# Three attentions run one step deeper, with divisions ahead of side work and output products inside the last step

## What is computed

```python
def first_block(...):                       # attention over 512 keys, spatial gating, 16 experts
    k_all = concat([kl, kc]); v_all = concat([vl, vc])
    mix_l = concat([gqa_attend(ql, k_all, v_all), spatial_gating(hl, ...)])
    xl_new = xl + gt1 * (mix_l @ w_out)
    xl_new = xl_new + gt2 * expert_choice_ffn(modulate(xl_new, g_ffn, sh2, sc2), w_router, w1, w3, w2)
    return rmsnorm(xl_new, g_final)

def mla_swa_layer(x, ...):                  # "even"
    o_mla = causal_block_attention(qm, km, v_m)
    o_swa = sliding_window_sink_attention(q_s, k_s, v_s, sinks, alibi_slopes(SWA_HEADS))
    return x + (concat([o_mla, o_swa]) * silu(gate)) @ w_out

def fox_layer(x, ...):                      # "odd"
    o = causal_block_attention(q, k, v, log_cum=log_cum)
    return x + (o * silu(gate)) @ w_out

def reference(...):
    x = first_block(...)
    x = mla_swa_layer(x, ...); x = fox_layer(x, ...)
    return rms_norm(x, g_final)
```

## Time and profile before

| | us |
|---|---|
| median of three runs | 1386.92 |
| the runs | 1386.84, 1386.92, 1388.49 |
| the profiled execution | 1388.61 |
| its span in the trace | 1386.8 |

### The profile page before, as it was taken

The page is one execution under the profiler, slowest core; times in us unless marked ns, Lnnn a source line. Parts: engine busy times, 40 slices in busy tenths (PEclk is TensorE's granted clock), DMA queues, the critical chain, the costliest instruction groups (busy, mean ns, idle before and its releaser), DMA issues.

```text
span 1386.8 us, 15261 instructions
## 1 busy us (share of the span) xinstructions
PE 992.9 (72%) x6623; PEld 510.2 (37%) x6623; DVE 396.3 (29%) x954; ACT 239.4 (17%) x483; POOL 89.6 (6%) x129
## 2 busy tenths in 40 slices
PE   4998987666666665566566565666656798899987
PEld 3765842212121111111111111111111487899875
DVE  4756421011111100101011010101101455775584
ACT  3534210000000000000000000000000355643452
POOL 1300000000020000000000000000000044300030
PEclk9999989878887887977888877788877798999998
DMA  9996789999999999999999999999999552144411
GB/s 398 375 378 237 317 362 428 428 429 426 429 427 427 430 427 427 429 427 428 429 428 427 428 428 426 430 428 427 428 427 428 216 184 98 62 182 146 159 62 46
DMA packets 34771, 482.47 MB, mean 348 GB/s; under 512 B 3854, under 2 KB 3856, under 8 KB 5520
## 3 DMA queue, kind: packets, MB, share of 16 engines
q1 hardware_dynamic: 34240, 479.92, 82.7%
q10 hardware_dynamic: 288, 1.05, 0.2%
q0 software_dynamic: 176, 0.53, 0.1%
HBM read 480.43 MB, written 1.05 MB: 347 GB/s over the span
## 4 chain that ended last, share of the span: by engine, by line
DMA 55%; PE 33%; DVE 6%; ACT 3%; issue 1%; POOL 1%; SPq 0%; POOLq 0%; DVEq 0%; ACTq 0%
DMA ring<-in_t_w 52%; PE PS L508 8%; PE PS L1009 6%; PE PS L496 6%; PE PS L1055 3%; DMA ring<-in_t_e_a 2%; DMA ring<-in_t_mod 2%; ACT S L624 1%; PE PS L690 1%; PE PS L485 1%; PE PS L997 1%; PE PS L786 1%; POOL RR L466 1%; PE PS L1022 1%; PE PS L808 1%
## 5 line engine op out<-in xcount | busy, mean ns | idle before, releaser
L1009 PE MATMUL PS<-ring,S 128*32 128x512 f32 x2016 | 320.7, 770 | 213.4 <-DMA ring<-in_t_w 210.9
L1055 PE MATMUL PS<-ring,S 128*32 128x512 f32 x1008 | 168.7, 803 | 103.7 <-DMA ring<-in_t_w 94.8
L1009 PEld LDWEIGHTS PS<-ring,S 128*32 128x32 f32 x2016 | 63.0, 126 | 447.7 <-DMA ring<-in_t_w 329.4
L514 DVE COPY S<-PS 128x512 f32<-128x512 f32 (+2 forms) x47 | 32.1, 682 | 307.9 <-PE PS L1055 287.7
L508 PE MATMUL PS<-SR,RR 128*128 128x256 f32 x736 | 117.5, 285 | 1.2 <-DVE ab L1441 0.9
L1055 PEld LDWEIGHTS PS<-ring,S 128*32 128x32 f32 x1008 | 33.3, 130 | 223.0 <-DMA ring<-in_t_w 147.6
L508 PEld LDWEIGHTS PS<-SR,RR 128*128 128x128 f32 x736 | 103.8, 189 | 2.6 <-DVE ab L1441 1.2
L454 ACT ACTIVATE RR<-ring 128x1024 fp32r<-128x1024 f32 (+3 forms) x95 | 89.5, 1005 | 37.8 <-DMA ring<-in_t_e_a 18.1
L1557 DVE TENSOR_SCALAR S<-PS,KC 128x256 f32<-128x256 f32 x16 | 7.7, 483 | 287.0 <-PE PS L1039 287.0
L516 ACT ACTIVATE S<-PS 128x512 f32<-128x512 f32 (+2 forms) x50 | 27.9, 568 | 340.8 <-PE PS L485 335.9
L466 DVE TENSOR_TENSOR RR<-ring,RR 128x1024 fp32r<-128x1024 f32 (+2 forms) x76 | 84.1, 1154 | 8.5 <-ACT RR L454 8.5
(11 more groups left out here) (309 smaller groups left out, 986.5 us busy)
## 6 DMA issues: line engine op xcount, KB each, us to landing
ring<-in_t_w SPq DMA_DIRECT2D x189, 2048.0 KB, 31.3
ring<-in_t_mod SPq DMA_DIRECT2D x12, 2048.0 KB, 12.7
ring<-in_t_out SPq DMA_DIRECT2D x6, 2048.0 KB, 7.8
S<-in_t_w SPq DMA_DIRECT2D x3, 2048.0 KB, 12.2
ring<-in_t_e_g SPq DMA_DIRECT2D x2, 2048.0 KB, 7.8
ring<-in_t_o_q SPq DMA_DIRECT2D x2, 2048.0 KB, 7.8
ring<-in_t_o_k SPq DMA_DIRECT2D x2, 2048.0 KB, 8.8
ring<-in_t_o_v SPq DMA_DIRECT2D x2, 2048.0 KB, 8.2
```

Source lines behind the costliest of these rows:

```text
L514: lane.e.tensor_copy(dst, src).then_inc(*lane.mark(out_of(key), *names))
L1009: m = pe.e.matmul(PS[32 * j:32 * j + 32, b, :], expert_rows(2 * k + kk, e_, e_ + 1), place[name, e_, k][:, kk, 512 * j:512 * j + 512], sta ...
L1055: m = pe.e.matmul(PS[q:q + 32, b, :], HT[e_ % 2][:, 128 * s + 32 * j:128 * s + 32 * j + 32], place["w2", e_, j][:, s, 512 * dh:512 * dh + ...
```

## The change

Four things are changed, none of them what is computed:

1. In all three attentions the scores, maxima and exponents of step 0 stand ahead of the loop (in the last two ahead of the gates' first pieces, together with the first division), and in round n those of step n+1 stand behind the transposes, copies and division of step n-1 and n. In the even attention the first step's patterns get two buffers of their own (`even_p`).
2. On VectorE the division stands ahead of the side work, and `gate_finish` stands behind it instead of at the head of the round.
3. In the last round of the even attention one block of the second output product stands between transposes and outputs (`out2_part`); in the odd attention half a block of the third (`out3_part`).
4. The blocks of the second and third output product come in another order (OUT2, OUT3), and VectorE's additions follow it.

```diff
-    A2_PB = [reg(o, 512) for o in (2048, 2560, 3072, 9216)]
+    A2_PB = [reg(o, 512) for o in (6144, 6656, 3072, 9216, 2048, 2560)]
+    def even_p(n, r):
+        return A2_PB[2 + (2 * n - 2 + r) % 4 if n else r]
+    OUT2 = ((1, 0), (1, 1), (0, 0), (0, 1), (1, 2), (0, 2), (1, 3), (0, 3))
+    OUT3 = ((1, 0), (0, 0), (1, 1), (0, 1))
...
         side = beside()
+        scores(0)
         for n in range(9):
-            if n < 8:
...
-            turn(side)
             if n:
                 for g in range(2):
                     pe.wait_ge((1, "p", n - 1, g))
                     transposes(pe, (1, "t", n - 1, g), ALL6,
                                [PB[(2 * (n - 1) + g) % 4][:, 128 * s:128 * s + 128] for s in range(4)])
+            if n + 1 < 8:
+                scores(n + 1)
             turn(side)
+            if n == 0:
+                turn(side)
             if n and n % 2 == 0:
...
+            if n:
+                turn(side)
         rest(side)
...
+        def out2_part(half, n2):
+            pe.wait_ge(*[("e", "done", m_) for m_ in ((0, 1) if half else (2, 3))])
+            straight(pe, ("out2", n2, half), ("out2", n2 // 2), OT, n2 % 2, final=half == 0 and n2 % 2 == 1,
+                     ks=range(4 * half, 4 * half + 4))
+
+        scores_even(0)
         side = gate_matmuls(pe, "e", (1, 0), HE)
...
+            scores_even(n + 1)
             turn(side)
+            if n == len(A2):
+                out2_part(*OUT2[0])
             if n:
...
+            turn(side)
         rest(side)
-        for half in (1, 0):
...
+        for half, n2 in OUT2[1:]:
+            out2_part(half, n2)
...
+        def out3_part(i, h, ks):
+            key, ukey = ("out3", h, i), ("out3", h)
...
+            for k in ks:
+                pe.wait_ge(("split", ukey, k), ("o", "done", (1 if i else 0) if k < 4 else (2 if i else 3)))
...
+            scores_odd(n + 1)
             turn(side)
+            if n == len(A3):
+                out3_part(*OUT3[0], range(4))
...
+            turn(side)
         rest(side)
+        out3_part(*OUT3[0], range(4, 8))
+        for i, h in OUT3[1:]:
+            out3_part(i, h, range(8))
...
+        maxima(0)
         for n in range(9):
+            if n:
+                probabilities_out(dve, n - 1, 1)
+            if n + 1 < 8:
+                maxima(n + 1)
             if n < 8:
...
+            turn(side)
             turn(side)
...
+        dve.wait_ge("bias")
+        largest_even(0)
+        divide_even(0)
         late = []
         side = gate_dve(dve, "e", (1, 0), late)
...
         for n in range(len(A2) + 1):
+            if n:
+                turned_out(dve, "e", n - 1, 1, A2_PT, 2)
+            largest_even(n + 1)
+            if n:
+                divide_even(n)
             gate_finish(dve, "e", late)
...
-            if n:
-                turned_out(dve, "e", n - 1, 1, A2_PT, 2)
-            if n < len(A2):
-                for r in range(2):
-                    divide(dve, "e", A2[n], n, r, A2_PB[(2 * n + r) % 4], sm2 if A2[n]["part"] == "mla" else sm3,
-                           columns(A2[n], r, 8), sinks=A2[n]["part"] == "swa")
...
+        for half, n2 in OUT2:
+            x3_add(n2, half)
+            if half == 0:
...
+                if n2 == 1:
+                    lo_all(dve, ("o", "q0"))
...
+        exponents_even(0)
         side = gate_act(act, "e", (1, 0), (("out2", 0), ("out2", 1)))
...
             if n:
                 turned_out(act, "e", n - 1, 0, A2_PT, 2)
+            exponents_even(n + 1)
```

More of the change, by code:

```diff
@@ L1165, in pe_program @@
                     values_flipped(pe, "e", A2[n - 1], n - 1, A2_PT, 2, lambda s, h: VM[:, s, h, :])
+            turn(side)
         rest(side)
-        for half in (1, 0):
-            pe.wait_ge(*[("e", "done", m_) for m_ in ((0, 1) if half else (2, 3))])
-            for n2 in range(4):
-                straight(pe, ("out2", n2, half), ("out2", n2 // 2), OT, n2 % 2, final=half == 0 and n2 % 2 == 1,
-                         ks=range(4 * half, 4 * half + 4))
+        for half, n2 in OUT2[1:]:
+            out2_part(half, n2)
         pe.stage("odd")
@@ L1225, in pe_program @@
                         score_mark(pe, m, "o", n, r, hh == len(step["heads"][0]) - 1)
+        def out3_part(i, h, ks):
+            key, ukey = ("out3", h, i), ("out3", h)
+            if ks[0] == 0:
+                banks.take(key, ALL6)
+                pe.wait_ge(banks.was[key])
+            for k in ks:
+                pe.wait_ge(("split", ukey, k), ("o", "done", (1 if i else 0) if k < 4 else (2 if i else 3)))
+                for n, (l_, r_) in enumerate(products(ukey, OT3, k, slice(0, 512), slice(128 * i, 128 * i + 128))):
+                    m = pe.e.matmul(PS[:, banks.of[key], :], l_, r_, start=(k == 0 and n == 0), stop=(k == 7 and n == 2))
+            if ks[-1] == 7:
+                m.then_inc(*pe.mark(key, *([used(ukey)] if i == 0 else [])))
+        pe.wait_ge(*[out_of((nm, n2)) for nm in ("q0", "q1", "k0", "k1") for n2 in range(2)], out_of("flT"), "kq")
+        scores_odd(0)
+        side = gate_matmuls(pe, "o", (0, 1), HO)
+        for _ in range(4):
             turn(side)
+        for n in range(len(A3) + 1):
             if n:
@@ L1783, in dve_program, with largest_odd @@
             copy_out(dve, ("x3t", i, 1), X[:, i, 512:1024], PS[:, banks.of["x3t", i, 1], :])
-        late = []
-        side = gate_dve(dve, "o", (0, 1), late)
-        for _ in range(4):
-            turn(side)
-        dve.wait_ge(out_of("cumulated"))
-        for n in range(len(A3) + 1):
-            gate_finish(dve, "o", late)
+        def largest_odd(n):
             if n < len(A3):
@@ L1796, in dve_program, with divide_odd @@
                             lambda h: cmask[:, 256 - nk:256], 0.125, shift=fl[:, step["i"], hs[0]:hs[-1] + 1:2])
+        def divide_odd(n):
+            if n < len(A3):
+                for r in range(2):
+                    divide(dve, "o", A3[n], n, r, A3_PB[(2 * n + r) % 4], sm4, columns(A3[n], r, 16))
+        dve.wait_ge(out_of("cumulated"))
+        largest_odd(0)
+        divide_odd(0)
+        late = []
+        side = gate_dve(dve, "o", (0, 1), late)
+        for _ in range(4):
+            turn(side)
+        for n in range(len(A3) + 1):
+            if n:
+                turned_out(dve, "o", n - 1, 1, A3_PT, 2)
+            largest_odd(n + 1)
+            if n:
+                divide_odd(n)
+            gate_finish(dve, "o", late)
             turn(side)
@@ L1937, in act_program, with exponents_mix @@
         act.wait_ge(out_of(("QT", 0)), out_of(("QT", 1)), out_of("KT"), "kr")
-        for n in range(9):
+        def exponents_mix(n):
             if n < 8:
@@ L1947, in act_program @@
                         *act.mark((1, "e", n, g), out_of((1, "s", n, g))))
-            turn(side)
+        exponents_mix(0)
+        for n in range(9):
             if n:
                 probabilities_out(act, n - 1, 0)
+            exponents_mix(n + 1)
+            turn(side)
             turn(side)
@@ L2059, in act_program, with exponents_even @@
         hi_all(act, ("e", "g0"))
+        def exponents_even(n):
+            if n < len(A2):
+                swa = A2[n]["part"] == "swa"
+                for r in range(2):
+                    exponents(act, "e", A2[n], n, r, even_p(n, r), nm3 if swa else nm2, sm3 if swa else sm2,
+                              columns(A2[n], r, 8), sinks=swa)
+        exponents_even(0)
         side = gate_act(act, "e", (1, 0), (("out2", 0), ("out2", 1)))
```

159 lines of the change are left out of this document (72 added, 87 removed).

## The result

| | before | after |
|---|---|---|
| median, us | 1386.88 | 1376.61 |
| the runs, us | 1386.84 to 1388.56 | 1372.41 to 1381.99 |
| profiled execution, us | 1388.61 | 1373.01 |
| its span, us | 1386.8 | 1371.2 |

The ratio is 0.9919, with a 95% interval of 0.9901 to 0.9937: 10.3 us or 0.8% faster. The forecast was 1376.3, the range 1370 to 1382. Two things warn against being content. So I read the trace by stages, between loads that both kernels issue at the same point of the work.

A forecast was written before the change was run, and what follows sets the result against it. The experts' weight stream bounds the middle; around it, TensorE's waits (22.6 us) are what can be won. First, even and odd attention gain 4.3 + 2.8 + 3.5 = 10.6 us: 1386.92 - 10.6 = 1376.3 us, range 1370 to 1382.

The forecast's parts named there:

- the term "1.4" for the clock: First attention: sixteen output matmuls ran at the lower clock behind a 2.64 us wait; 1.4 us to be gained.
- Rival 3: The experts' weight stream swallows the first attention's gain; 6.3 us gained in all, 1380.6 us; chance 0.07.
- (a): Even attention: first step's scores go ahead of the gates, where TensorE waits for GpSimd; 1.2 us gained, the rest hidden.
- I set both at nothing: Even attention: fewer holes could keep the clock high, the new 2.9 us wait could lower it; both priced at zero.
- the bank argument: Even attention: the next gate product needs the bank the gate's finish frees, so TensorE waits 2.9 us instead of 0.6.
- Part (e): Even attention, last step: 2.8 us of output product between transposes and outputs remove the wait of 2.0 us.
- The condition that I named for GpSimd being the loser: Even attention: if VectorE's early work slows GpSimd, the loop starts up to 2 us later; total gain 8.6 us.
- transposes 4: Odd attention: these transposes wait 2.1 us, since VectorE's maxima take 4 us a step beside GpSimd's conversions.
- Rival 1: The waits vanish almost wholly, new ones being covered; 17 us gained, 1369.9 us; chance 0.15.
- Rival 2: Waits only change names in the last two loops; 4.3 us gained, the first attention alone, 1382.6 us; chance 0.11.
- Rival 4: Slower: new waits bring low clock in the loops, up to 43 us lost, 1391 us with 30; chance 0.03.
- Rival 5: Gains and new waits cancel over the whole kernel, 1386.9 us; chance 0.04.

The follow-up runs named there:

- e2: The kernel before with the even attention's change alone, second output product included; ratio 1.0008 to the kernel before.
- e4: The changed kernel run again unaltered, for a second profile and more runs; ratio 0.9926 to the kernel before.
- e3: The kernel before with the odd attention's change and the third output product alone; ratio 0.9975 to the kernel before.
- e5: The changed kernel with the gate's finish ahead of the next step's maxima in both last loops; ratio 0.9891 to the kernel before.
- e7: The changed kernel with first output products behind the last step again; 0.9950 to the kernel before. Its Theory B: VectorE's copy stands first, so 1 to 2 us slower.

## Why the prediction was right, and where it was not

The number is right in part by luck. By stages of the profiled executions, which leave the entry's clock out, the change brings 6.5 - 1.1 + 4.4 = 9.8 us; the medians say 10.3; forecast were 4.3 + 2.8 + 3.5 = 10.6. The even attention was 3.9 us too high, the other two together 3.1 too low, and of these 3.1 half is clock that came in this pair of executions and not in all.

**First attention: right in kind, in this pair 2.2 us too low** (6.5 for 4.3, in its bounds). The four steps with one piece of modulation were to wait 2.0 us; there are three such waits, 0.49, 0.79 and 0.49. The wait of the third output product was 0.84 for 1.3, that of the last modulation column 0.8 for 0.7. The 0.9 us of hand-overs are not in the trace: I charged them on top of steps whose chains were counted through already. The clock gave 1.9 instead of 1.4 us (TensorE's busy time up to the load at 154.6 or 148.3 fell from 63.8 to 61.9).

But this clock is not the change's. e2 has the old first attention with the same wait of 2.64 us ahead of the same outputs, and they took 1.95 us there, not the 3.35 of the earlier trace rows. The changed kernel has a slow place too, in its second profile (e4): 24 matmuls took 4.62 us that took 3.11 in the first, at 127.44.

```profile
108.29 1.95 PE L931 MATMUL PS<-S 128*64 128x256 f32 x16 [2.64 <-ACT S L516]
...
127.41 4.62 PE L508 MATMUL PS<-SR,RR 128*128 128x256 f32 x24
```

From the loop's first scores to that load it is 71.2 and 71.4 us with the old loop (before, e3) at 0.98, and 69.8 (e2) at 1.00; with the new loop it is 65.1 us in six profiles at 1.00 and 66.5 to 66.6 in five at 0.97. Between executions of like clock the change brings 4.6 to 4.7 us. So the term "1.4" for the clock stood on a single execution, the new waits were put 1.5 us too high (4.9 for 3.4), and the two errors cancel: that the forecast of 4.3 lies so near is luck. The DMA swallowed nothing: from the release to the load e_a it took 872.3 us after 873.8, so Rival 3 is out.

**Even attention: wrong, and outside its bounds** (1.1 us lost, bounds -0.5 and 6; in e2, with the wait ahead of the transposes at 1.57 us, 0.5 gained). The step that failed is (a), "VectorE and ScalarE stand idle there, so maxima, exponents and division of that step are hidden". The maxima were hidden. But ScalarE was not idle: 5.3 us of conversions and table load stood ahead of the exponents, and VectorE waited 2.67 us for them. The division that followed ran into the gate's product and cost the 2.07 us ahead of the transposes: I had priced small operations beside GpSimd at 0.5 us more each, and left out that the eight divisions of 128 x 128 slow down as well. The groups of instructions show them beside GpSimd after, and mostly away from it in the loop before (mean ns in the last column but for the idle time):

```profile
L646 DVE TENSOR_SCALAR S<-S,st 128x128 f32<-128x128 f32 x8 | 5.1, 701 | 0.1
...
L639 DVE TENSOR_SCALAR S<-S,st 128x128 f32<-128x128 f32 x16 | 3.5, 282 | 0.1
```

The second failed step is the clock, "I set both at nothing": TensorE was busy 2.2 us longer. The wait for the gate's finish was right to 0.2 us (3.07 for 2.9), and e5 confirms the bank argument. But a wait longer than one behind which the clock had been low before deserved a price of its own, at least as a bound. The small terms held: 0.68 for the transposes of step 4 (0.5 forecast), 0.55 for its outputs (0.6); the wait for a division beside GpSimd (0.4) and the hand-overs (0.3) did not come. Part (e) held: no wait in the last step, and e7 prices it, though at 1.1 us of wait and not 2.0; e7 keeps VectorE's copy early, which its Theory B gives as the reason.

The condition that I named for GpSimd being the loser did not occur. Its 32 conversions took 22.56 us before, without step 0 beside them, and 22.57 after. So where the Trainium skill (SBUF — State Buffer, Who interferes with whom) has either engine blocked by the other, here VectorE alone paid.

**Odd attention: 4.4 for 3.5 us gained.** New waits of 4.2 us instead of the 6.4 forecast: 1.15 ahead of scores 2 (1.6), 1.7 ahead of transposes 3 (1.2), 0.76 ahead of transposes 4 (2.1), 0.55 ahead of outputs 4 (0.7), none at step 2 (0.8). The mis-sized term is transposes 4. I let the small operations behind the maxima take 0.66 us in every step from GpSimd's start on; they did so in one step and in half of the next:

```profile
1321.41 0.44 DVE L618 SCALAR_TENSOR_TENSOR S<-S,st 128x2 f32<-128x2 f32 x1
1321.89 0.65 DVE L620 SCALAR_TENSOR_TENSOR S<-S,st 128x2 f32<-128x2 f32 x1
1323.26 0.67 DVE L618 SCALAR_TENSOR_TENSOR S<-S,st 128x2 f32<-128x2 f32 x1
1323.96 0.66 DVE L620 SCALAR_TENSOR_TENSOR S<-S,st 128x2 f32<-128x2 f32 x1
...
1330.32 0.66 DVE L620 SCALAR_TENSOR_TENSOR S<-S,st 128x4 f32<-128x4 f32 x1
...
1332.39 0.17 DVE L620 SCALAR_TENSOR_TENSOR S<-S,st 128x4 f32<-128x4 f32 x1
```

The waits account for the whole gain. The 1.4 us of clock did come (the stretch stands at 1.00), but TensorE's busy time fell by 0.2 us only. A part of what took them are matmuls just behind a wait: the transposes behind the 1.7 us wait took 1.38 us, others 1.03. The rest stays open. The tail is unchanged at 6.7 us.

**Rivals.** Of Rival 1, the vanishing waits, only the odd loop's late steps have something. Rival 2, that waits only change names in the last two loops, holds for the even loop (e2), not for the odd (e3). Rival 4, the clock, holds in small: it took 2.2 us and not 21. Rival 5, that gains and new waits cancel, is excluded for the whole by the interval and holds for the even attention alone.

**The range**, 1370 to 1382, held the median and the six runs of the comparison, but its width came from the sizes of the waits. The entry's clock, at up to 7.8 us in a single execution, was in no term of it, nor the 1.5 us of the first attention's.

## What to carry to other kernels

Taking one step ahead into another engine's idle time is free only for engines that are idle to its end: follow the moved work through every engine to its last instruction (here ScalarE's conversions delayed it by 2.67 us), and look at which bank, copy or product queues behind it. Work that frees a PSUM bank (here the gate's finish, 0.7 us) is worth trying ahead of work that is needed a step later: moving it back ahead gave 8.5 us by the stages, nearly as much as the whole change's 9.8. A cost that was read from one execution, like the 1.4 us of clock, wants a second one before it becomes a term of a sum. And where runs of one kernel differ by more than the effect, compare stage by stage between events that both kernels share.

## What the hardware showed that I had not expected

- TensorE's granted clock in a stretch that no edit touches differs between executions of one kernel: the even layer's entry took 26.1 and 32.7 us in two profiles of the changed kernel, at 0.93 and 0.69. Keeping TensorE busy ahead of it (22.3 of 23.2 us) did not prevent a clock of 0.75 there.
- The clock behind one and the same wait differed between executions: behind 2.64 us the same sixteen matmuls took 3.35 us and 1.95.
- Behind long waits the clock was low in the even loop, beside the waits' length: 0.60 behind two waits of 2.1 and 3.1 us a few us apart, 0.83 behind one of 4.1, 1.00 behind one of 2.2. In the even stage of the changed kernel TensorE's busy time was 3.5 us above that of e5, more than the 3.1 us of idle time between them.
- Beside GpSimd's conversions VectorE's division of 128 x 128 took 0.70 us instead of 0.28, small operations of 128x2 and 128x4 mostly 0.44 to 0.78 instead of 0.16 to 0.19, while GpSimd's own 32 conversions did not change by more than 0.01 us in 22.6.
